# A two-layer encoder with a top-2-of-8 mixture of experts: experts sorted into positions with 96 or 64 token slots, weights fetched from an address read at run time

## What is computed

```python
def moe_swiglu(h, w_router, w_gu, w_down):
    ht = h.reshape(b * s, d)                       # 256 x 1024
    logits = (ht @ w_router).astype(jnp.float32)   # 256 x 8
    top_val, top_idx = lax.top_k(logits, TOP_K)    # TOP_K = 2
    top_w = jax.nn.softmax(top_val, axis=-1)
    gates = jnp.sum(jax.nn.one_hot(top_idx, N_EXPERTS, dtype=jnp.float32) * top_w[..., None], axis=1)
    out = jnp.zeros_like(ht)
    for e in range(N_EXPERTS):
        out = out + gates[:, e:e + 1] * swiglu(ht, w_gu[e], w_down[e])
    return out.reshape(b, s, d)

def swiglu(h, w_gu, w_down):
    g, u = jnp.split(h @ w_gu, 2, axis=-1)
    return (jax.nn.silu(g) * u) @ w_down
```

## Time and profile before

| | us |
|---|---|
| median of 3 runs | 1521.18 |
| lowest and highest | 1517.09, 1524.14 |
| profiled execution, its own time | 1525.58 |
| its span in the trace | 1523.8 |

### The profile page before, as it was taken

How to read it: one execution, slowest core, us unless ns; L and a number is a source line. 1 busy time by engine, 2 the same in 40 slices (tenths; PEclk the granted TensorE clock), 3 DMA queues, 4 the chain that set the end, 5 groups by cost and what they waited for, 6 DMA issues and landing times.

```text
span 1523.8 us, 33668 instructions
## 1 busy us (share of the span) xinstructions
PE 1479.8 (97%) x15677; PEld 926.7 (61%) x15677; DVE 486.4 (32%) x692; ACT 348.3 (23%) x509; POOL 101.2 (7%) x127
## 2 busy tenths in 40 slices
PE   5999999999999999799999999999999999999997
PEld 4898889999888888535435435335335335345344
DVE  3775685555568568310010010010010010020121
ACT  4445754333454565200000000000000000000000
POOL 4412000010122000300000000000000000000000
PEclk9999999999999999999999999999999999999999
DMA  9545455755545337899999999999999999999993
GB/s 294 176 147 139 135 193 194 240 178 191 194 156 176 120 109 316 326 326 418 417 388 418 417 386 418 418 385 418 412 391 418 399 403 418 396 402 419 413 418 122
DMA packets 134738, 468.82 MB, mean 308 GB/s; under 512 B 10113, under 2 KB 66593, under 8 KB 105921
## 3 DMA queue, kind: packets, MB, share of 16 engines
q1 hardware_dynamic: 131280, 456.44, 77.8%
q0 software_dynamic: 2176, 6.29, 1.8%
q10 hardware_dynamic: 1136, 3.87, 0.7%
HBM read 460.67 MB, written 9.05 MB: 308 GB/s over the span
## 4 chain that ended last, share of the span: by engine, by line
PE 93%; DVE 4%; DMA 2%; POOL 1%; ACT 1%; issue 0%; SPq 0%; DVEq 0%; ACTq 0%; POOLq 0%
PE bank L1694 38%; PE bank L1716 19%; PE bank L1391 11%; PE bank L1392 10%; PE bank L1393 10%; DMA w_slot<-in_w_in 2%; PE bank L1427 1%; PE bank L1456 1%; DVE w_slot_lo L485 1%; PE bank L1442 1%; PE bank L1642 0%; PE bank L1652 0%; PE bank L1513 0%; DVE probT_rope L1055 0%; DVE gate_area L1078 0%
## 5 line engine op out<-in xcount | busy, mean ns | idle before, releaser
L1694 PE MATMUL bank<-w_slot,a 128*32 128x512 f32 (+1 forms) x5376 | 508.3, 539 | 0.7 <-ACT a L975 0.7
L1694 PEld LDWEIGHTS bank<-w_slot,a 128*32 128x32 f32 x5376 | 179.2, 110 | 324.1 <-issue 322.9
L485 DVE TENSOR_TENSOR w_slot_lo<-w_slot,w_hi_lo 128x2048 fp32r<-128x2048 f32 (+1 forms) x93 | 212.2, 2289 | 114.0 <-ACT w_hi_lo L478 113.3
L478 ACT CAST w_hi_lo<-w_slot 128x2048 fp32r<-128x2048 f32 (+1 forms) x93 | 173.9, 1877 | 133.5 <-PE bank L1393 117.4
L1304 DVE TENSOR_TENSOR a<-a,bank 128x512 f32<-128x512 f32 (+1 forms) x16 | 9.9, 620 | 535.4 <-PE bank L1694 535.4
L1716 PE MATMUL bank<-w_slot,b 128*32 128x256 f32 x3072 | 168.7, 379 | 0.0
L1716 PEld LDWEIGHTS bank<-w_slot,b 128*32 128x32 f32 x3072 | 100.5, 110 | 65.9 <-issue 3.0
L1391 PE MATMUL bank<-w_hi_lo,a_lo 128*128 128x512 f32 x312 | 125.3, 402 | 12.1 <-DVE w_slot_lo L485 6.3
L1391 PE MATMUL bank<-b_lo,w_hi_lo 128*128 128x256 f32 x448 | 127.3, 284 | 0.5 <-DVE b_lo L1031 0.5
L1392 PE MATMUL bank<-b_lo,w_hi_lo 128*128 128x256 f32 x448 | 127.2, 284 | 0.0
L1393 PE MATMUL bank<-b_lo,w_slot_lo 128*128 128x256 f32 x448 | 127.1, 284 | 0.0
(11 more groups left out here) (176 smaller groups left out, 1282.1 us busy)
## 6 DMA issues: line engine op xcount, KB each, us to landing
w_slot<-in_moe_w_gu SPq DMA_DIRECT2D x112, 1024.0 KB, 17.4
w_slot<-in_moe_w_gu SPq DMA_DIRECT2D x112, 768.0 KB, 17.5
w_slot<-in_moe_w_down SPq DMA_DIRECT2D x80, 1024.0 KB, 17.0
w_slot<-in_w_in SPq DMA_DIRECT2D x44, 1024.0 KB, 5.0
w_slot<-in_ffn_w_gu SPq DMA_DIRECT2D x22, 1024.0 KB, 5.1
w_hi<-in_moe_w_gu SPq DMA_DIRECT2D x16, 1024.0 KB, 19.9
w_slot<-in_moe_w_down SPq DMA_DIRECT2D x32, 512.0 KB, 17.5
w_hi<-in_moe_w_down SPq DMA_DIRECT2D x16, 1024.0 KB, 19.0
```

The costliest lines, as they stand in the source:

```text
L478: nc.scalar.copy(hi_slot[n % HI_RING][:, 0:WIDTH[n]], raw[:, 0:WIDTH[n]]).then_inc(hi_ready, 1)
L485: eng.tensor_tensor(lo, raw, hi, ALU.subtract).then_inc(lo_ready, 1)
L1694: last = nc.tensor.matmul(bank[first_bank + b][s * TOKENS:(s + 1) * TOKENS, 0:width], pickedT[:, c, b * TOKENS:(b + 1) * TOKENS], w[:, s * ...
```

## The change

Item p is no longer expert p. Position 0 stays expert 0. Experts 1 to 7 are sorted on chip by token count. Positions 1 and 7 have 64 slots and take the two experts with the fewest tokens; positions 2 to 6 have 96 slots (`CAPS`). At 64 slots there are two token groups instead of three, in the matmuls, in silu, product and transposes, in the copies of the output, and in the rows loaded and stored.

VectorE computes the sort in a new function, `sort_experts`. It gives each expert its position and its capacity, and each position its expert number `who`. GpSimd needs position and capacity for the row numbers. SyncE reads one entry of `who` for each of positions 1 to 7 into a register and forms the addresses of that position's 48 weight loads from it. An expert that exceeds its position's capacity triggers the second round, as before with 96. With the counts above, the two smallest of experts 1 to 7 have 54 and 56 tokens.

```diff
-ROUNDS = -(-SEQ // SLOTS)
+CAPS = (96, 64, 96, 96, 96, 96, 96, 64)
+ROUNDS = 1 + -(-(SEQ - min(CAPS)) // SLOTS)
+GROUPS = [cap // TOKENS for cap in CAPS]
+def y_order(groups):
+    return (2, 0, 1) if groups == TOKEN_GROUPS else (0, 1)
...
 # SyncE
-                for e in range(EXPERTS - 1 if first else 0):
-                    load_rest(first_item + e, e, True)
-                    load_first(first_item + e, e + 1)
-                    sp.wait_ge(y_copied, (first_item + e) * 2 + 4)
...
+                    expert = 0
+                    for p in range(EXPERTS - 1):
+                        load_rest(p, expert, True)
+                        sp.wait_ge(who_ready, 1)
+                        expert = sp.value_load(who[0:1, p + 1:p + 2], min_val=0, max_val=EXPERTS - 1)
+                        load_first(p, expert)
+                        sp.wait_ge(y_copied, p * 2 + 4)
+                        rows = by_expert(y_rows)[p][0:CAPS[p], :].rearrange("(b p) n -> p b n", p=TOKENS)
...
-                load_rest(first_item + (EXPERTS - 1), EXPERTS - 1)
+                load_rest(first_item + (EXPERTS - 1), expert)
...
 # GpSimd
-            own(nc.gpsimd.tensor_scalar(row_at, iota8.unsqueeze(1).broadcast_to([P, BLOCKS, EXPERTS]),
+            pool.wait_ge(ranks_ready, 1)
+            pool.wait_ge(position_ready, 1)
+            ranks = rank_x.rearrange("p e b -> p b e")
+            own(nc.gpsimd.tensor_scalar(row_at, position.unsqueeze(1).broadcast_to([P, BLOCKS, EXPERTS]),
                                         float(ROWS), None, ALU.mult))
...
-            own(nc.gpsimd.tensor_scalar(rank, ranks, float(SLOTS), 2.0 * NO_ROW, ALU.is_ge, ALU.mult))
+            own(nc.gpsimd.tensor_tensor(rank, ranks, cap.unsqueeze(1).broadcast_to([P, BLOCKS, EXPERTS]), ALU.subtract))
+            own(nc.gpsimd.tensor_scalar(rank, rank, 0.0, 2.0 * NO_ROW, ALU.is_ge, ALU.mult))
...
 # VectorE
+            def sort_experts():
+                dve.wait_ge(expert_rank, 1)
+                own(nc.vector.scalar_tensor_tensor(out=key, in0=count, scalar=float(EXPERTS), in1=iota8,
+                                                   op0=ALU.mult, op1=ALU.add))
+                own(nc.vector.memset(key[:, 0:1], float(2 * EXPERTS * SEQ)))
+                own(nc.vector.tensor_tensor(pairs, key.unsqueeze(1).broadcast_to([P, EXPERTS, EXPERTS]),
+                                            key.unsqueeze(2).broadcast_to([P, EXPERTS, EXPERTS]), ALU.is_lt))
+                own(nc.vector.tensor_reduce(order, pairs, AX_X, ALU.add))
...
+                own(nc.vector.tensor_tensor(position, order, lowest, ALU.add))
+                own(nc.vector.tensor_tensor(position, position, highest, ALU.subtract))
+                nc.vector.scalar_tensor_tensor(out=margin, in0=count, scalar=float(SLOTS), in1=cap,
+                                               op0=ALU.add, op1=ALU.subtract).then_inc(position_ready, 1)
...
+                nc.vector.tensor_copy(who[:, :], key).then_inc(who_ready, 1)
...
             def first_picks(item, first):
-                choose_tokens(item, 0)
+                choose_tokens(rank_x[:, 0, :])
+                if first:
+                    sort_experts()
...
 # TensorE, gate and up
-                        for b in range(TOKEN_GROUPS):
+                        for b in range(groups):
...
 # TensorE, down
-                    for b in Y_ORDER:
+                    for b in order:
                         for n in range(n_chunks):
                             for s in range(STREAMS):
```

More of the change, by code:

```diff
@@ L64 @@
 TOKEN_GROUPS = SLOTS // TOKENS
+GROUPS = [cap // TOKENS for cap in CAPS]
+SMALL = [p for p in range(EXPERTS) if CAPS[p] < SLOTS]
+UNWRITTEN = [p for p in SMALL if p < EXPERTS - 1]
+Y_ZEROED = 16 * (1 + len(UNWRITTEN))
 STREAMS = 4
@@ L464, in y_place, with units, y_units @@
             return bank[(6, 7, 2)[b]][:, 0:Y_STREAM]
+        def units(item, first):
+            if first:
+                return PARTS * sum(GROUPS[:item])
+            return item * (PARTS * TOKEN_GROUPS) - PARTS * (EXPERTS * TOKEN_GROUPS - sum(GROUPS))
+        def y_units(item, first):
+            return 0 if first else (on_chip(item) - 1) * TOKEN_GROUPS - (TOKEN_GROUPS - GROUPS[-1])
         def on_chip(item):
@@ L1295, in first_picks @@
             def first_picks(item, first):
-                choose_tokens(item, 0)
+                choose_tokens(rank_x[:, 0, :])
+                if first:
+                    sort_experts()
             def expert(item, e, more, first):
+                groups = GROUPS[e] if first else TOKEN_GROUPS
                 def act_product(part):
                     dve.wait_ge(w_used, moe_used(item, MOE_PLACE[("u", part, DC - 1)]))
-                    for b in range(TOKEN_GROUPS):
-                        dve.wait_ge(silu_done, item * (PARTS * TOKEN_GROUPS) + (part * TOKEN_GROUPS + b + 1))
+                    for b in range(groups):
+                        dve.wait_ge(silu_done, units(item, first) + (part * groups + b + 1))
@@ L1306, in act_out @@
                 def act_out(part):
-                    for b in range(TOKEN_GROUPS):
-                        dve.wait_ge(act_ready, item * (PARTS * TOKEN_GROUPS) + (part * TOKEN_GROUPS + b + 1))
+                    for b in range(groups):
+                        dve.wait_ge(act_ready, units(item, first) + (part * groups + b + 1))
                         nc.vector.transpose(actT[part][:, b], act_cols(b, part).rearrange("p (t c) -> p c t", t=TOKENS))\
@@ L1662, in expert @@
                 scatters = not (first and more)
+                groups = GROUPS[e] if first else TOKEN_GROUPS
+                order = y_order(groups)
                 def places():
@@ L1737, in expert @@
                     return
-                pe.wait_ge(y_ready, on_chip(item) * TOKEN_GROUPS)
+                pe.wait_ge(y_ready, y_units(item, first) + groups)
                 for t in range(BLOCKS):
-                    for b in range(TOKEN_GROUPS):
+                    for b in range(groups):
                         for y in (y_hi, y_lo):
```

143 lines of the change are left out of this document (89 added, 54 removed).

## The result

The changed kernel takes 1508.8 us (median of four runs, 1508.1 to 1511.9) against 1519.3 us for the kernel before. The ratio of the runs is 0.9932, with a 95% interval of 0.9914 to 0.9951: some 10.3 us faster. The forecast was 1510.3 us, 10.9 less than the 1521.2 known then. The profiled execution took 1511.87 us, its span is 1510.1.

What follows compares the result with a forecast made beforehand. TensorE and the weight loads were taken as nearly level bounds, with little TensorE lead left. 8.7 + 1.6 + 0.6 = 10.9 us off 1525.6 gave 1514.7 profiled, 1510.3 us with the 4.4 offset; range 1495 to 1518.

Steps and rivals of the forecast that it cites:

- Two bounds nearly level: Per full item, 109.4 us of TensorE matmuls against about 111.8 us of loads, so most saved matmul time becomes waiting.
- Rival 1: Items 1 and 7: the saved TensorE time comes off in full, 73 us, giving 1448; 1 in 100.
- rival 5: Weight loads run faster than read, at up to 421 GB/s, ending 33 us sooner; halfway is 1494; 10 in 100.
- 8.7 us from the end of the queue: End of item 7: TensorE ends at 1503.2 instead of 1511.9, one 1.7 us tile after the last landing at 1501.5.
- 1.6 us from less in the queue: Load queue: 0.6 us for fewer rows stored and loaded, 1.0 us from position 7's shorter token load.
- 0.6 us from the tail: After the last tile: one group fewer saves a copy, a difference and a third of the scatter matmuls, 0.6 us.
- The offset: The median of unprofiled runs was assumed to stay 4.4 us below the profiled execution, turning 1514.7 into 1510.3.
- The sort, SyncE and ScalarE at nothing: Sort ahead of the experts, SyncE's reads and extra load instructions, ScalarE's shorter work: all hidden, cost 0.
- rival 3: SyncE can't issue loads in time, deciding from 1.9 us extra a load; 54 us slower, 1575; 3 in 100.
- TensorE's waits: Idle for weight loads: 10 to 15 us in position 1, 1 to 5 in each of 2 to 6, 35 to 40 in 7.
- The clock: In positions 1 and 7 a waiting TensorE, 65% busy, might drop to half clock; no cost taken, up to 3 us at the end.

Runs made afterwards that it cites:

- e4_before_cut: Kernel before, with each 768 KB gate and up tile loading only 512 KB and the matmuls unchanged; ratio 0.9989 to the kernel before.
- e5_after_cut: Changed kernel, with each 768 KB gate and up tile loading only 512 KB and the matmuls unchanged; 1459.5 us, ratio 0.9598 to the kernel before.
- e2_only7: Changed kernel with only position 7 at 64 slots, position 1 back at 96; 1513.0 us, ratio 0.9946 to the kernel before.
- e3_only1: Changed kernel with only position 1 at 64 slots, given the smallest expert, position 7 at 96; 1514.5 us, ratio 0.9955 to the kernel before.
- e1_all96: Changed kernel with all eight positions at 96 slots, sort and run-time addresses kept; 1520.3 us against 1520.5 for the kernel before, ratio 0.9990.
- e6_017: Changed kernel with position 0 at 64 slots too, so positions 0, 1 and 7 are small; 1506.1 us, ratio 0.9902 to the kernel before.

## Why the prediction was right

**Two bounds nearly level.** This mechanism carried the forecast, and it is confirmed by `e4_before_cut` and `e5_after_cut`: the same shorter loads are worth 0 in one kernel and 50.8 us in the other. Rival 1's 1448 would have needed landings 62 us sooner, and rival 5 a pace of 421 GB/s; the last landing came 1.2 us sooner after item 0's first matmul, at 405 GB/s on average.

**8.7 us from the end of the queue.** The wait of the last tile fell from 7.8 to 0.04 us, and TensorE's end behind the last landing from 10.4 to 2.0, 8.4 us; the last tile took 1.98 us where 1.7 were expected. `e2_only7` and `e3_only1` show that either position is enough to bring TensorE to the newest landing.

**1.6 us from less in the queue.** From item 0's first matmul to the last landing it was 1501.5 - 636.3 = 865.2 us, and is 1498.0 - 634.0 = 864.0: 1.2. Profiles of kernels with nearly the same loads differ by as much, so the term as a whole is neither shown nor refuted. Its largest part, 1.0 us for a third fewer token rows, finds no support in the trace: over the 17 us up to 1 us behind its landing, the changed kernel's last token load, of 64 rows, leaves 351 GB/s (1321.3 to 1338.3), and item 3's, of 96 rows, 350 (986.2 to 1003.2).

**0.6 us from the tail.** The three terms shrank by 0.56 us, from 2.15 to 1.59.

**The offset.** The profiled execution came out 2.8 us below its forecast of 1514.7, 2.3 of them from ahead of the experts, and lies 3.1 above the median where 4.4 were assumed. That the median is met to 1.5 us is in part luck, within the 5 us kept for it.

**The sort, SyncE and ScalarE at nothing.** `e1_all96` confirms it within 0.3%. GpSimd's last scatter was issued 9.3 us after the ranks (628.8 to 638.1) and is now 12.2 after them, 2.9 later where 3.2 were expected. The reads of `who` take 0.3 us each, less than the few us I allowed, and the extra instructions 0.07 us a load where rival 3 needed 1.9.

**TensorE's waits.** 10.3 us of idle in item 1 and 1.5 in item 3 are as forecast. Item 7 shows 27.9 where I wrote 35 to 40, and TensorE's busy time fell by 57.8 where I wrote 70. Item 7 takes 110.2 us for matmuls worth 72.9 at full pace, so 37.3 us were lost. The 9.4 us between are counted as busy, because a tile between two waits is recorded longer than its share of a stream of tiles: the last tile's 32 records take 1.98 us by themselves and 32 x 54.3 ns = 1.74 at full pace. The items' starts were the safe measure, not the idle column.

**The clock.** It stayed at 1.00 from 632 to 1506 us in the changed kernel, though the matmuls of items 1 and 7 fill only 72.9 of their 87.6 and 110.2 us. What the Trainium skill, "TensorE: Matmul & The Clock Gate", section "HAM oscillation — how this bites in real kernels", tells of a kernel that ran cold behind each of its waits for DMA was seen once in the experts' stretches of these profiles, in item 1 of `e6_017`. There it cost nothing, because TensorE at 1.2 GHz worked without a pause and was granted 2.4 GHz again after 3.4 us.

## What to carry to other kernels

An engine that is busy for 100% of a stretch is not the bound that pays, if a second resource is busy for 100% too: compare the two paces over one period (109.4 us of matmuls, 111.5 of loads) and take the lead that is left at the end (here 7.8 us, and 0.9 for the shorter last tile) as the most that relief of the first can bring. A growing time from issue to landing shows which resource is behind, long before anything waits. After such a change look at the new bound: here two small edits, of when transfers run and on which queue, took some 14 us more.

## What the runs showed of the hardware

Around a load of 96 rows of 4 KB among loads of 768 KB on one queue, the sixteen engines stayed busy (share 1.02) but moved 329 GB/s instead of 421 for 14 us. The same load, issued earlier and on ScalarE's queue, brought them to 366 GB/s for 8.9 us; one of 16 rows on SyncE's queue to 403 for 14. The time ahead of the experts, which no variant was meant to shorten, ranged from 628.4 to 641.4 us, more than the effect of the change; a stretch within the trace resolved what single totals could not.
